# Half of k of two column blocks per MLP part as seven half-chunk products (Strassen's scheme), the weight sums made by accumulating DMA

## What is computed

```python
MLP_HIDDEN = 4 * D_MODEL          # D_MODEL = 2048, SEQ = 256

def _sq_relu_mlp(h, w_up, w_down):
    a = jax.nn.relu(h @ w_up)
    return (a * a) @ w_down

# in first_block, after the mixer:
h = h + _sq_relu_mlp(_rmsnorm(h, mlp_norm[i]), mlp_w_up[i], mlp_w_down[i])
```

## Time and profile before

| | |
|---|---|
| time, median of 3 runs | 2489.48 us (2489.32 to 2491.32) |
| span of the profiled execution | 2489.0 us |
| PE, busy | 2476.7 us, 100% of the span |
| DVE, busy | 1505.6 us, 60% |
| ACT, busy | 1554.5 us, 62% |
| POOL, busy | 33.4 us, 1% |
| ring's DMA queue, share of the 16 engines | 51.7% |

### The profile page before, as it was taken

One profiled execution on the slowest core, in us unless ns is written; L12 is line 12 of the kernel. 1 busy time (PEld: TensorE's weight loads), 2 busy tenths in 40 slices (PEclk: granted clock), 3 DMA queues, 4 the chain that ended last, 5 costly groups with the idle time before them and its releaser, 6 DMA issues.

```text
span 2489.0 us, 29742 instructions
## 1 busy us (share of the span) xinstructions
PE 2476.7 (100%) x12451; PEld 2046.9 (82%) x12451; DVE 1505.6 (60%) x1267; ACT 1554.5 (62%) x2078; POOL 33.4 (1%) x41
## 2 busy tenths in 40 slices
PE   9999999999999999999999999999999999999998
PEld 7887788888888888888878888888888888888887
DVE  5775656545545545676765675545566667646675
ACT  6635777636637547776465585445587688638873
POOL 0000000000000000000000000000000000000000
PEclk9999999999999999999999999999999999999999
DMA  8554555555555555545443455555655555555554
GB/s 288 188 201 164 185 198 188 199 188 196 193 192 197 188 201 187 198 174 188 154 152 142 159 179 185 199 188 196 260 191 183 186 190 199 188 199 188 197 192 152
DMA packets 69366, 472.37 MB, mean 190 GB/s; under 512 B 7912, under 2 KB 8352, under 8 KB 13424
## 3 DMA queue, kind: packets, MB, share of 16 engines
q1 hardware_dynamic: 67040, 460.62, 51.7%
q0 software_dynamic: 1312, 7.73, 0.8%
q10 hardware_dynamic: 880, 2.11, 0.2%
HBM read 468.33 MB, written 2.11 MB: 189 GB/s over the span
## 4 chain that ended last, share of the span: by engine, by line
PE 97%; DVE 1%; ACT 1%; issue 1%; DMA 0%; SPq 0%; POOLq 0%; POOL 0%; DVEq 0%; ACTq 0%
PE acc L526 31%; PE acc L528 31%; PE acc L527 31%; PE tp L810 1%; PE tp L743 0%; PE tp L546 0%; DMA w_raw<-in_stream 0%; DVE w_lo L1662 0%; PE tp L682 0%; ACT w_hi L1024 0%; PE tp L691 0%; DVE cv L1946 0%; ACT xp L1543 0%; PE tp L561 0%; PE tp L562 0%
## 5 line engine op out<-in xcount | busy, mean ns | idle before, releaser
L1662 DVE TENSOR_TENSOR w_lo<-w_raw,w_hi 128x2048 fp32r<-128x2048 f32 x430 | 983.7, 2289 | 715.0 <-ACT w_hi L1024 713.1
L1024 ACT ACTIVATE w_hi<-w_raw 128x2048 fp32r<-128x2048 f32 x430 | 823.1, 1916 | 482.7 <-DMA w_raw<-in_stream 466.6
L526 PE MATMUL acc<-w_hi,x_hi 128*128 128x512 f32 (+1 forms) x2240 | 874.8, 391 | 0.8 <-DVE w_lo L1669 0.4
L528 PE MATMUL acc<-w_hi,x_lo 128*128 128x512 f32 (+1 forms) x2240 | 868.4, 388 | 0.0
L527 PE MATMUL acc<-w_lo,x_hi 128*128 128x512 f32 (+1 forms) x2240 | 868.3, 388 | 0.0
L526 PEld LDWEIGHTS acc<-w_hi,x_hi 128*128 128x128 f32 x2240 | 420.7, 188 | 90.6 <-issue 2.6
L528 PEld LDWEIGHTS acc<-w_hi,x_lo 128*128 128x128 f32 x2240 | 420.6, 188 | 86.6
L527 PEld LDWEIGHTS acc<-w_lo,x_hi 128*128 128x128 f32 x2240 | 420.8, 188 | 85.2 <-issue 1.0
L526 PE MATMUL acc<-w_hi,a_hi 128*128 128x512 f32 x1120 | 436.4, 390 | 0.1
L527 PE MATMUL acc<-w_lo,a_hi 128*128 128x512 f32 x1120 | 435.7, 389 | 0.0
L528 PE MATMUL acc<-w_hi,a_lo 128*128 128x512 f32 x1120 | 435.7, 389 | 0.0
(11 more groups left out here) (386 smaller groups left out, 1320.3 us busy)
## 6 DMA issues: line engine op xcount, KB each, us to landing
w_raw<-in_stream SPq DMA_DIRECT2D x430, 1024.0 KB, 4.8
w_raw<-in_stream SPq DMA_DIRECT2D x16, 256.0 KB, 7.4
h<-in_x SPq DMA_DIRECT2D x4, 512.0 KB, 14.8
frow<-in_rows POOLq DMA_DIRECT2D x2, 1024.0 KB, 7.0
m_raw<-in_mem_turned POOLq DMA_DIRECT2D x1, 2048.0 KB, 11.4
memt<-in_mem POOLq DMA_DIRECT2D x1, 2048.0 KB, 10.7
x_raw<-in_x_turned SPq DMA_DIRECT2D x3, 512.0 KB, 7.6
dec<-gc_rows ACTq DMA_DIRECT2D x1, 1024.0 KB, 6.9
```

The source lines that it names most:

```text
L526: pe.matmul(dst, xh, wh[:, k], start=first and k == 0, stop=False)
L528: mm = pe.matmul(dst, xl, wh[:, k], start=False, stop=last and k == n_k - 1)
L1024: act.activation(w_hi[:, c % SLOTS], w_raw[:, c % SLOTS], ACT.Copy).then_inc(hi_ready, 1)
L1662: dve.tensor_tensor(w_lo[:, c % SLOTS], w_raw[:, c % SLOTS], w_hi[:, c % SLOTS].bitcast(F32), ALU.subtract).then_inc(lo_ready, 1)
```

## The change

**The scheme.** In each part the up blocks n = 2 and 3 are called left and right. Their first half of k (q = 0, 1) is computed as before by row halves and quarters: a 2 x 2 product of (row half m) x (quarter q) with (quarter q) x (block), which took eight half-chunk products (a half-chunk: one chunk, one row half, 12 matmuls). Now seven half products do it, by the Winograd form of Strassen's scheme. Three (11, 13, 16) use a weight chunk as it is and four a sum of weight chunks (T1 to T4); 9, 11 and 13 use rows of x as they are and the other four a sum of such rows (`s_hi`, `s_lo`). The second half of k (q = 2, 3) stays as ordinary chunks. So a part has 35 items instead of 32 chunks: 0 to 7 ordinary (blocks 0 and 1), 8, 10, 14, 18 ordinary chunks of the pair, 9, 11, 12, 13, 15, 16, 17 half products, 19 to 34 the down product. Items 9, 12, 15, 17 read T4, T1, T2, T3, which don't pass through the ring; each has a buffer of its own.

**The weight sums.** POOL loads the first chunk of a sum from HBM and adds one to three more by DMA (`accum_op=ALU.add`), each after the one before has landed. T1 and T3 have two chunks, T2 three and T4 four: 11 transfers of 1 MB a part, 7 of them adding. T2 and T4 of the next part start when item 17 is done, T1 and T3 at the start of the part.

**The partial sums.** Products that serve several outputs are gathered in a PSUM bank of `tp` (chain) and one in its neighbour (both). ACT copies the chain out after items 13, 15 and 17 (`chain_taken`), DVE adds the accumulators and both into `nat`, and ACT then scales `nat` in place (`pair_scaled`). Blocks 2 and 3 are so completed together at items 17 and 18, no longer one after the other. The down product now runs in the order `LATER(4)`: (0,0), (0,1), (0,2), (1,0), (1,1), (1,2), (0,3), (1,3), then blocks 2 and 3.

**Around it.** In part 0 DVE forms the sums of x (`sums_of_x`, steps 2, 3 and 6). In part 3 the steps of the next norm move with the new order. The load of `frow` moves from POOL's queue ahead of the MLP to item 10 of the last part. Some semaphores are shared.

```diff
+        SUM_AT = {9: "T4", 12: "T1", 15: "T2", 17: "T3"}
+        SUM_OF = {"T1": ((0, 0), (0, 1)), "T2": ((0, 0), (0, 1), (1, 1)), "T3": ((0, 1), (1, 1)), "T4": ((0, 0), (0, 1), (1, 0), (1, 1))}
+        UP_AT = {8: (2, 2), 10: (3, 2), 11: (1, 2), 13: (0, 2), 14: (2, 3), 16: (1, 3), 18: (3, 3)}
...
-            for c in range(SLOTS, NCHUNK):
-                sp.wait_ge(used, c - SLOTS + 1)
-                sp.dma_start(w_raw[:, c % SLOTS], stream[c]).then_inc(landed[c % SLOTS], 16)
+            for n in range(SLOTS, len(RING)):
+                c = RING[n]
+                sp.wait_ge(used, RING[n - SLOTS] + 1)
+                sp.dma_start(w_raw[:, n % SLOTS], stream[source(c)]).then_inc(landed[n % SLOTS], 16)
...
+            def first_of_sum(t, g):
+                pool.dma_start(sum_raw[t][:], part_of(t, g, 0)).then_inc(sum_in[t], 16)
+
+            def add_to_sum(t, g, n):
+
+                pool.wait_ge(sum_in[t], 16 * (len(SUM_OF[t]) * g + n))
+                pool.dma_start(sum_raw[t][:], part_of(t, g, n), accum_op=ALU.add).then_inc(sum_in[t], 16)
...
             norm(1, 2)
+            for g in range(GROUPS):
+                if g:
+                    pool.wait_ge(used, C_MLP + GROUP * (g - 1) + 18)
+                    first_of_sum("T2", g)
+                    first_of_sum("T4", g)
+                    add_to_sum("T2", g, 1)
+                    add_to_sum("T4", g, 1)
+                add_to_sum("T2", g, 2)
+                add_to_sum("T4", g, 2)
+                add_to_sum("T4", g, 3)
+                pool.wait_ge(used, C_MLP + GROUP * g)
+                first_of_sum("T1", g)
+                first_of_sum("T3", g)
+                add_to_sum("T1", g, 1)
+                add_to_sum("T3", g, 1)
...
+            def product(c, xh, xl, dst, start=False, stop=False):
+
+                pe.wait_ge(lo_ready, ready(c))
+                wh = w_hi[:, c % SLOTS].rearrange("p (k n) -> p k n", n=N)
+                wl = low_part(c).rearrange("p (k n) -> p k n", n=N)
+                for k in range(4):
+                    pe.matmul(dst, xh[:, k], wh[:, k], start=start and k == 0, stop=False, skip_group_check=True)
+                    pe.matmul(dst, xh[:, k], wl[:, k], start=False, stop=False, skip_group_check=True)
+                    mm = pe.matmul(dst, xl[:, k], wh[:, k], start=False, stop=stop and k == 3, skip_group_check=True)
+                mm.then_inc(used, 1)
...
+                chunk(c0 + 8, X, 8, left, True, False)
+                product(c0 + 9, *of_x(1, 1), acc[:, left % 2, 1])
+                chunk(c0 + 10, X, 12, left, False, True)
+                product(c0 + 11, *of_x(1, 0), acc[:, left % 2, 0], stop=True)
...
+                product(c0 + 12, *of_s(0), both, start=True, stop=True)
+                if g:
+                    pe.wait_ge(pair_out, pair_step(g - 1, "p7"))
+                product(c0 + 13, *of_x(0, 0), chain, start=True, stop=True)
+                chunk(c0 + 14, X, 8, right, True, False)
+                pe.wait_ge(pair_out, pair_step(g, "p1"))
+                product(c0 + 15, *of_s(1), chain, stop=True)
+                product(c0 + 16, *of_s(3), acc[:, right % 2, 0])
+                pe.wait_ge(pair_out, pair_step(g, "p6"))
+                product(c0 + 17, *of_s(2), chain, stop=True)
+                chunk(c0 + 18, X, 12, right, False, True)
...
+                for c in range(16):
+                    b, q = LATER(4)[c]
+                    if b == 0:
                         pe.wait_ge(a_low, 4 * g + q + 1)
+                    chunk(C_MLP + GROUP * g + 19 + c, A, 4 * q, accs.name["down", g, b], q == 0, q == 3)
...
+                    chain_taken(part, c)
+                    if c == 20:
+                        squares_moved(4 * part + 2, 2)
+                    if c in (21, 22):
+                        squares_moved(4 * part + 3, 2 * (c - 21))
...
+                    split(C_MLP + GROUP * part + c + AHEAD)
+                    if c == 18:
+                        pair_scaled(part, 2)
+                    if c == 19:
+                        pair_scaled(part, 3)
+                        squares_moved(4 * part + 2, 0)
...
+                    if c in (19, 20):
+                        n = c - 17
+                        if n == 2:
+                            blk = accs.name["up", part, 3]
+                            dve.wait_ge(used, C_MLP + GROUP * part + 19)
+                            dve.tensor_tensor(nat[:, 1], nat[:, 1], acc[:, blk % 2], ALU.add).then_inc(accs.sem(blk), 1)
+                        dve.wait_ge(pair_out, pair_step(part, f"up{n}"))
+                        dve.wait_ge(sq_moved, 4 * part + n - 1)
+                        dve.transpose(turned[n % 2][:], nat[:, n % 2].rearrange("p m n -> p (m n)")).then_inc(nat_turned, 1)
...
+                    if c in (5, 9, 21, 23):
+                        n = (5, 9, 21, 23).index(c)
                         dve.wait_ge(a_high, 4 * part + n + 1)
```

More of the change, by code:

```diff
@@ L74, in build @@
         a_lo = sb("a_lo", [P, 16, SEQ], F32R, a_a + 16 * K)
+        a_sh = take(8 * K)
+        s_hi = sb("s_hi", [P, 4, 4, P], F32R, a_sh)
+        x_sum = sb("x_sum", [P, 2, 4, SEQ], F32, a_sh)
         a_nat = take(8 * K)
@@ L219, in tpf @@
             return tp[:, g % 2].rearrange("p k t -> p (k t)")
-        landed = [sem(f"landed{s}") for s in range(SLOTS)]
         hi_ready, lo_ready, used = sem("hi_ready"), sem("lo_ready"), sem("used")
@@ L230, in build @@
         x_in = sem("x_in")
-        w_part = [[sem(f"w_part{c}_{k}") for k in range(4)] for c in range(EARLY)]
+        w_part = [[sem(f"w_part{c}_{k}") for k in range(3)] for c in range(EARLY)]
+        landed = [sem(f"landed{s}") for s in range(SLOTS)]
+        for c in range(EARLY):
+            w_part[c].append(landed[c])
         gain_in, xT_in, x0_high, x0_low = sem("gain_in"), [sem(f"xT_in{n}") for n in range(NB + 1)], sem("x0_high"), sem("x0_low")
@@ L295, in build @@
             for n in range(4):
-                accs.add(("up", g, n), "act")
+                accs.add(("up", g, n), "act" if n < 2 else "dve")
             for n in range(4):
@@ L327, in landing @@
         def landing(c):
-            return 16 * (c // SLOTS + (1 if c % SLOTS >= EARLY else 0))
+            return 16 * (c // SLOTS + 1)
         for b in range(6):
@@ L660, in _, with up_pair, of_x, of_s @@
                 gla_side(48 + c)
-            for g in range(4):
-                for c in range(32):
+            def product(c, xh, xl, dst, start=False, stop=False):
[7 more added lines that the diff above has]
+                mm.then_inc(used, 1)
+            def up_pair(g):
+                c0, left, right = C_MLP + GROUP * g, accs.name["up", g, 2], accs.name["up", g, 3]
+                chain, both = tpf(0)[:, 0:N], tpf(0)[:, N:2 * N]
+                def of_x(q, m):
+                    return [t[:, 4 * q:4 * q + 4, m * P:(m + 1) * P] for t in X]
+                def of_s(n):
+                    return s_hi[:, n], s_lo[:, n]
+                chunk(c0 + 8, X, 8, left, True, False)
+                product(c0 + 9, *of_x(1, 1), acc[:, left % 2, 1])
+                chunk(c0 + 10, X, 12, left, False, True)
+                product(c0 + 11, *of_x(1, 0), acc[:, left % 2, 0], stop=True)
+                if g == 0:
+                    pe.wait_ge(s_formed, 2)
+                    tps.wait(pe, tps.name["s", 3])
+                    tps.wait(pe, tps.name["o", 3])
+                product(c0 + 12, *of_s(0), both, start=True, stop=True)
[9 more added lines that the diff above has]
+                chunk(c0 + 18, X, 12, right, False, True)
+            for g in range(GROUPS):
+                for c in range(8):
                     b, q = divmod(c, 4)
@@ L1018, in split @@
             def split(c):
-                if c < NCHUNK:
-                    act.wait_ge(landed[c % SLOTS], landing(c))
+                if c < NITEM:
+                    if sum_of(c):
+                        act.wait_ge(sum_in[sum_of(c)], summed(c))
+                    else:
+                        act.wait_ge(landed[PLACE[c] % SLOTS], landing(PLACE[c]))
                     if c >= SLOTS:
                         act.wait_ge(used, c - SLOTS + 1)
-                    act.activation(w_hi[:, c % SLOTS], w_raw[:, c % SLOTS], ACT.Copy).then_inc(hi_ready, 1)
+                    act.activation(w_hi[:, c % SLOTS], raw(c), ACT.Copy).then_inc(hi_ready, 1)
             def split_part(c, k):
@@ L1884, in _ @@
                             half_carried(("norm3", 3), sq[1][:], turned[1][:])
-                    if part == 3 and c in (22, 26, 30):
-                        norm_low(3, c // 4 - 5, COL["norm_mix"])
-                    split(C_MLP + 32 * part + c + AHEAD)
+                    if part == 3 and c - 19 in (9, 11, 14):
+                        norm_low(3, (9, 11, 14).index(c - 19), COL["norm_mix"])
+                    split(C_MLP + GROUP * part + c + AHEAD)
+                    if c == 18:
```

(7 more changed lines are left out.)

149 lines of the change are left out of this document (112 added, 37 removed).

## The result

The changed kernel takes 2563.09 us (median of 4 runs, 2561.84 to 2564.51), the kernel before 2490.31 us beside it (4 runs, 2489.32 to 2491.32): ratio 1.0292, 95% interval 1.0279 to 1.0304, so 72.8 us more. Forecast were 2540 us, range 2515 to 2565, slower. The profiled execution took 2561.84 us; its span is 2560.0, against 2489.0. In what follows the runs of a batch have their own median of before: 2491.25 for the first four experiments, 2490.99 and 2491.06 for the others.

What follows compares the result with a forecast made beforehand. PE was taken to bound the kernel. Per part -2.7 + 0.9 + 10.3 + 2 (clock) + 2 (contention) = +12.5, times 4 = +50, and 1 once, gave 2540 us from 2489.5; range 2515 to 2565.

Steps and rivals of the forecast that it cites:

- the rival with long traffic: Accumulating transfers delay ring loads of items 21 to 28 to 12 us; item 21 waits 17.6; 2565 us, chance 0.13.
- 48 matmuls less: Seven half products replace eight, saving PE 12 matmuls or 2.72 us per part, 10.9 us in all.
- order at item 21, with the clock: At the down product's item 21, PE waits 10.3 us for a_lo, plus 2 us clock loss, in every part.
- item 12: At item 12, PE waits 0.9 us per part for the low part of its split.
- contention and late sums: Sums' transfers beside split 22's load cost 2 us per part; T4's late last adds in part 0 cost 1 once.
- The queue worked out: From item 17's end, ACT and DVE finish a_lo at 26.6 us; PE, free at 16.3, waits 10.3.
- The clock: After item 21's stall PE returns at the lower clock, costing 2 us per return, bounds 0 and 3.8.
- Contention: POOL's T2 and T4 transfers delay split 22's load after item 17: 2 us per part, bounds 0 and 3.3.
- the doubled add: A DMA add reads two sources, twice the read traffic, so lands some 3 us later than a copy.
- Late sums in part 0: T4's last two adds follow POOL's rstd in part 0 and may reach ACT late: 1 us once.
- the bound of 14: Upper bound in us for one add of the sums to land, everything done twice; 10 was taken.
- The rest costs nothing: DVE's sums of x and ACT's s_hi fit idle time in items 2 to 6; uncovered, 9 us once.

Runs made afterwards that it cites:

- the first four experiments: Four edits of the changed kernel: DVE's a_lo earlier; block 2 first in both queues; adds left out; PE fed throwaway matmuls: 2547.72, 2523.32, 2533.78, 2555.06 us.
- complete version: Changed kernel with block 2 first in ACT and DVE, sums' transfers one at a time, item 12's split before half of block 1's squares: 2484.70 us.
- Experiments 1 and 2: Against the changed kernel: 1, DVE takes block 2's low part before item 23's split, 2547.72 us; 2, block 2 first in ACT and DVE, 2523.32 us.
- experiment 10: Changed kernel with block 2 first in ACT's and DVE's queues and the sums' transfers one at a time from item 22: 2489.70 us.
- experiment 11: The complete version: 2484.70 us, ratio 0.9976 to the kernel before.
- experiment 6: Changed kernel with the sums' transfers one at a time, T4 and T2 from item 22, in part 0 whole before the norm: 2537.85 us.
- experiment 5: Changed kernel with block 2 first in ACT and DVE, the 28 adds left out and the 16 loads issued singly: 2486.18 us.

## Why the prediction was right, and where not

Right were the sign, the mechanism and the place. 2563 lies in the range, but at its end, 23 us above the likeliest value and beside the 2565 of the rival with long traffic: that it is inside at all is owed to the width of the range, since one term was nearly three times too small. The rival had the ring's loads land after 12 us; at 470 to 500 they do so after 10.1 (median), 4.8 before; but item 21 waited 14.0 and not 17.6 us, and item 25 not at all. The terms, measured one after another from the changed kernel to the complete version (the four medians come from three batches, whose kernels before differ by up to 0.8 us):

| term | predicted | measured |
|---|---|---|
| 48 matmuls less | -10.9 | -10.9 by 48 steps of 0.227; not measured alone |
| order at item 21, with the clock | 4 x (10.3 + 2) = 49.2 | 2537.85 - 2489.70 = 48.2 |
| item 12 | 4 x 0.9 = 3.6 | 2489.70 - 2484.70 = 5.0 |
| contention and late sums | 4 x 2 + 1 = 9 | 2563.09 - 2537.85 = 25.2 |
| left over | 0 | 72.8 + 10.9 - 78.4 = 5.3 |

- **Order.** The queue worked out gave 10.3 us; where no sums are made beside it the wait was 10.1 to 10.3 (part 3 of six kernels). Experiments 1 and 2 took it away in two pieces.
- **The clock.** 2 us for each return; 1.7, 2.0, 2.8 and 1.8 in the changed kernel's trace. Not foreseen was that waits of 2.0 and 2.5 us can pull the clock down too (last section).
- **Item 12.** 0.9 taken, 0.74 to 0.77 seen, and 1.87 in part 0. With the first matmuls after a wait, which come 0.2 to 0.3 us late in all on top of the idle time shown, the term is 1.2 a part: 4.7 us in the MLP between the profiled executions of experiments 10 and 11, though 1.2 more lie ahead of the MLP, where both have the same instructions.
- **Contention is the step that failed in size.** "Bounds 0 and 3.3 per part ... so I take 2": item 21 alone lost 3.9 (14.0 against 10.1), beyond the upper bound, and items 6 to 10 of the parts, which the sum had at nothing, waited for another 1.8 us in part 0 (1.21 and 0.54), 1.4 in part 1, 0.3 in part 2 and 0.4 in part 3. In part 0 split 22's load ended ACT's wait at 487.88, 14.1 us after the end of item 17, where the queue had 10.1 and the sum 2 more. The bound came from a plain 2 MB copy, 3.3 us; two of the sums' transfers side by side go beyond it. The prediction had the two numbers that warn, the ring's 51.7% and the doubled add, but used the second for landing times alone. Where the ring needs half of the engines, a second stream that never pauses and pays double per packet takes more than the other half (61.8% against 39.3% in the stretch above).
- **Ahead of the MLP** the sum had no term, and 6.0 us were lost there: T2's and T4's first four transfers (303 to 330) lie beside loads that then land after 9.4 us (median) instead of 4.7. With them one at a time 3.7 are left in experiment 6 and 2.4 in 11.
- **Late sums in part 0** were to cost 1 us; part 0 lost 5.6 more than part 1. The 28 adds landed after 9.1 to 17.9 us, median 12.8 where 10 was taken: the bound of 14 was too low for two side by side. What it did is in the changed kernel's rows:

```profile
432.73 1.92 ACT L1159 ACTIVATE w_hi<-raw_T 128x2048 fp32r<-128x2048 f32 x1 [1.96 <-DMA raw_T<-in_stream]
434.68 2.29 DVE L1831 TENSOR_TENSOR lo_T<-raw_T,w_hi 128x2048 fp32r<-128x2048 f32 x1 [3.39 <-ACT w_hi L1159]
436.89 2.28 DVE L2046 TENSOR_TENSOR s_lo<-s_raw,s_hi 128x2048 fp32r<-128x2048 f32 x1
439.10 1.24 DVE L2058 STREAM_TRANSPOSE turned<-nat 128x1024 f32<-128x1024 f32 x1
440.26 2.25 DVE L1831 TENSOR_TENSOR w_lo<-w_raw,w_hi 128x2048 fp32r<-128x2048 f32 x1
442.56 0.79 PE L612 MATMUL acc<-w_hi,x_hi 128*128 128x512 f32 x1 [2.51 <-DVE w_lo L1831]
```

  T4's last add lands late and ACT stands idle 1.96 us for it. DVE then has T4's low part, `s_lo` and a transpose in front of item 10's low part, though ACT had finished item 10's high part at 437.6. So item 10's wait of 2.51 us, with 1.7 us of slow steps behind it, comes from T4 and the order in DVE's queue and not from item 10's own load. With T4 whole ahead of the norm (experiment 6) item 10 waits no more.
- **"The rest costs nothing"** held where T4 was in time: experiment 5 has it all, and shows no wait that it could have made. Behind a late T4, `s_lo` lengthened the wait (rows above).
- The gains don't add up singly: order alone brings 39.8 us, singling alone 25.2, both 73.4. With item 21 mended, items 24 and 25 meet the late ring; with the ring mended they don't.

The 5.3 us left over are not settled. 0.7 of them is the difference of two medians of the kernel before (2490.31 and 2490.99). By the profiled executions of before and experiment 11, and after the 10.9 us saved, 1.7 us lie ahead of the MLP (it starts at 381.05 instead of 379.33), 4.3 in it and -1.2 behind it; of the 4.3 the four short waits at item 21 are 2.6, with their late first steps. The adds, even one at a time, cost about 3.5 (experiment 10 against 5): by the profiled executions 2.3 ahead of the MLP and 2.1 in it. Nothing was tried against either.

## What to carry to other kernels

Where a bound engine has a few microseconds of reserve per step, work out the queues of the other engines instruction by instruction when a change makes two results ready together: here one instruction that waited for its load held a finished block for 9 us, and the order of a few instructions was worth 48 us where the saved work was worth 11. Count a background transfer by its share of the DMA engines and not only by its landing time, and try such transfers one at a time if the foreground stream needs half of the engines: here the sums' transfers cost 29 us side by side (2563.1 against 2533.8) and 4 singly (2537.9 against 2533.8). An edit that seems too small may be held back by another; try pairs before giving one up.
